# Table powers between projection steps, the convolution in 14 of 16 slots, a wait ahead of the expert splits

## The reference

```
h = rms_norm(x, g_mix);  z = h @ w_in
c_val, c_gate, s_in = z[:, :512], z[:, 512:1024], z[:, 1024:]
y_conv = silu(layer_norm(causal_conv31(c_val * sigmoid(c_gate)) + conv_b))
y_ssm  = s5_ssm(s_in, ...)      # 32 groups of 16 channels, 64 complex states each
x = x + [rms_norm(y_conv), rms_norm(y_ssm)] @ w_out
x = x + hierarchical_moe(rms_norm(x))     # 4 groups x 8 experts, top 2, SwiGLU
return rms_norm(x, g_final)
```

## Time and profile before

| | |
|---|---|
| median of 3 runs | 1887.34 us (1884.49 to 1889.06) |
| profiled execution | 1895.12 us, of it 1893.7 in the span of the trace |
| PE busy | 1640.9 us, 87% of the span |
| DVE, ACT, POOL busy | 1116.7 (59%), 803.3 (42%), 605.9 (32%) |
| mean granted PE clock | 0.924 of full speed |
| stages, from the trace | projection to 360, convolution and state space to 545, mix to 918, experts to 1847, final norm to the end |

### The profile page before, as it was taken

The page is one execution under the profiler, slowest core; times in us unless marked ns, Lnnn a source line. Parts: engine busy times, 40 slices in busy tenths (PEclk is TensorE's granted clock), DMA queues, the critical chain, the costliest instruction groups (busy, mean ns, idle before and its releaser), DMA issues. The chain is left out here.

```text
span 1893.7 us, 33245 instructions
## 1 busy us (share of the span) xinstructions
PE 1640.9 (87%) x11171; PEld 1500.2 (79%) x11172; DVE 1116.7 (59%) x1707; ACT 803.3 (42%) x1022; POOL 605.9 (32%) x882
## 2 busy tenths in 40 slices
PE   7699999688937999999269999999999999999970
PEld 7599999577827888888268999899999888989860
DVE  7845564244547566665617646654666886665546
ACT  3222221012245333342315646644665775665543
POOL 0776774222323336444311212121222121212120
PEclk9899999878968898989579999999999999999995
DMA  8544342498854224312539878885877999887749
GB/s 278 169 146 147 127 161 85 121 223 247 225 200 137 97 89 134 101 67 90 215 119 316 275 240 272 274 285 188 291 273 257 382 366 359 280 275 254 261 137 366
DMA packets 166974, 403.90 MB, mean 213 GB/s; under 512 B 67967, under 2 KB 103169, under 8 KB 140417
## 3 DMA queue, kind: packets, MB, share of 16 engines
q1 hardware_dynamic: 140320, 336.26, 49.7%
q0 software_dynamic: 20080, 58.34, 12.7%
q10 hardware_dynamic: 6512, 8.51, 1.4%
HBM read 313.92 MB, written 89.13 MB: 213 GB/s over the span
## 5 line engine op out<-in xcount | busy, mean ns | idle before, releaser
L1637 DVE TENSOR_TENSOR expert_lo<-expert_raw,expert_hi 128x2048 fp32r<-128x2048 f32 x192 | 430.5, 2284 | 46.4 <-ACT expert_hi L1633 44.6
L1633 ACT CAST expert_hi<-expert_raw 128x2048 fp32r<-128x2048 f32 x192 | 361.6, 1910 | 18.1 <-DMA expert_raw<-in_experts 9.8
L720 PE MATMUL proj_p_z<-proj_x_hi,proj_w_hi 128*128 128x256 f32 x768 | 222.2, 289 | 14.1 <-DVE proj_x_lo L553 14.1
L721 PE MATMUL proj_p_z<-proj_x_lo,proj_w_hi 128*128 128x256 f32 x768 | 218.7, 285 | 0.0
L722 PE MATMUL proj_p_z<-proj_x_hi,proj_w_lo 128*128 128x256 f32 x768 | 218.5, 285 | 0.0
L2037 PE MATMUL moe_p_g0u<-expert_hi,moe_xh 128*128 128x256 f32 x736 | 210.8, 286 | 1.5 <-DVE moe_xl L1950 1.5
L2039 PE MATMUL moe_p_g0u<-expert_lo,moe_xh 128*128 128x256 f32 x736 | 206.6, 281 | 0.0
L2038 PE MATMUL moe_p_g0u<-expert_hi,moe_xl 128*128 128x256 f32 x736 | 206.6, 281 | 0.0
L2052 PE MATMUL moe_p_y<-expert_hi,moe_hh 128*128 128x512 f32 x368 | 153.4, 417 | 13.1 <-DVE moe_hl L1961 13.1
L1879 POOL DMA_INDIRECT residual<-moe_y,moe_ids_s x46 | 78.5, 1708 | 265.6 <-ACT moe_y L1906 258.1
L720 PEld LDWEIGHTS proj_p_z<-proj_x_hi,proj_w_hi 128*128 128x128 f32 x768 | 148.9, 194 | 14.2 <-issue 14.1
(11 more groups left out here) (416 smaller groups left out, 4149.9 us busy)
## 6 DMA issues: line engine op xcount, KB each, us to landing
expert_raw<-in_experts SPq DMA_DIRECT2D x192, 1024.0 KB, 6.2
ffn_input<-mix_h SPq DMA_DIRECT2D x17, 512.0 KB, 3.9
proj_x_sb<-in_x SPq DMA_DIRECT2D x8, 1024.0 KB, 7.3
mix_x_sb<-in_x SPq DMA_DIRECT2D x16, 512.0 KB, 5.0
residual<-mix_x SPq DMA_DIRECT2D x16, 512.0 KB, 2.7
out<-final_x SPq DMA_DIRECT2D x16, 512.0 KB, 6.4
proj_x_raw<-in_x_turned SPq DMA_DIRECT2D x7, 1024.0 KB, 4.8
proj_w_raw<-in_w_in SPq DMA_DIRECT2D x8, 768.0 KB, 7.3
```

The source lines that it names most:

```text
L720: nc.tensor.matmul(o, whi, x_hi[:, half, c], start=start, stop=False)
L721: nc.tensor.matmul(o, whi, x_lo[:, half, c], start=False, stop=False)
L1633: self.nc.scalar.copy(self.hi[:, u], self.raw[:, u]).then_inc(self.hi_done, 1)
L1637: tensor_tensor(self.lo[:, u], self.raw[:, u], self.hi[:, u].bitcast(FP32), ALU.subtract).then_inc(self.lo_done, 1)
```

## The change

It has three parts. No arithmetic changes, and no operation is added or left out, but the eight signed copies of the powers move from DVE to ACT.

**Projection.** `table_factors` is split: `powers` runs after `low(2)` and `factors(2)`, ahead of the scaling of step 1; ACT makes the signed copies (`signed_powers`); `scaled_b` runs after step 1. All loops are written out. The group t of unit j in step n is now `t = (n - 2) * 6 + j - 2`: tables begin at unit 2 of step 2. `expand` follows the scaling of the unit with a pair's second group, and `skip_lag` follows the scaling of the unit after that, which for a pair in units 4 and 5 is unit 0 of the next step.

```diff
+        def group_at(n, j):
+            t = (n - FIRST) * UNITS + j - FIRST_UNIT
+            return t if 0 <= t < GRP else None
...
+            def signed_powers():
+                act.wait_ge(powers_done, 1)
+                ...
+                    last = nc.scalar.activation(to[half].rearrange("p g j -> p j g"), of[half], ACT.Copy, scale=float(sign))
+                last.then_inc(signed, 1)
...
             def factors(n):
                 dve.wait_ge(squared, n * 2 + 2)
+                wait(dve, spread, n)
...
+            def body(n, half):
+                if 1 < n < T8 - 1:
+                    low(n + 1, 1 - half)
+                    factors(n + 1)
+                for j in range(UNITS):
+                    if j >= 4:
+                        glu(n, j - 4)
+                    scaled(n, half, j)
+                    t = group_at(n, j)
+                    if t is not None and t % PAIR == PAIR - 1 and t + 1 < GRP:
+                        expand(t // PAIR + 1)
+                    before = group_at(n, j - 1) if j else group_at(n - 1, UNITS - 1)
+                    if before is not None and before % PAIR == PAIR - 1:
                         for g in range(PAIR):
+                            skip_lag(before // PAIR, g)
                 for j in (2, 3):
                     glu(n, j)
-            body(0, 0, False, 0)
-            table_factors()
-            body(1, 1, True, 0)
-            expand(0, 0)
+            body(0, 0)
+            low(2, 0)
+            factors(2)
+            powers()
+            body(1, 1)
+            scaled_b()
+            dve.wait_ge(signed, 1)
+            expand(0)
+            for n in range(2, T8):
+                body(n, n % 2)
```

```diff
+        TWICE = (5, 9)
+        banks_in = [[0]]
+        for m in range(1, SLOTS):
+            after = banks_in[-1][-1] + 1 if banks_in[-1] else CT * BANKS
+            banks_in.append(list(range(after, min(after + (2 if m in TWICE else 1), CT * BANKS))))
...
+            load_in(0)
             load_u(0)
-            load_column(nc, sp, bias[:, :], conv_b).then_inc(b_in, 16)
-            load_in(0)
             sp.wait_ge(tables_st, 16 * TB)
             load_toep(0)
...
             load_toep(1)
+            sp.dma_start(bias[:, :], conv_b).then_inc(b_in, 16)
             load_u(2)
...
             for m in range(SLOTS):
-                bank(m)
+                for i in banks_in[m]:
+                    bank(i)
...
             act.wait_ge(b_in, 16)
             for m in range(SLOTS):
-                copy_bank(m)
-                if m % BANKS == 2 and m > 2:
-                    finish(m // BANKS - 1)
+                for i in banks_in[m]:
+                    copy_bank(i)
+                if tile_ending(m - 2) is not None:
+                    finish(tile_ending(m - 2))
                 copy_y(m)
-            finish(CT - 1)
```

```diff
-            pool.sem_inc(entries_issued, 1)
             pool.wait_ge(scattered_last, 16 * 2 * LT)
...
-            dve.wait_ge(entries_issued, 1)
+            dve.wait_ge(scattered_last, 16 * 2 * LT)
```

More of the change, by code:

```diff
@@ L368, in _, with body @@
             u_v = scratch["u"].rearrange("(c p) s k -> s p c k", p=P)
-            def body(n, half, more, pairs):
+            def body(n, more):
                 if more:
@@ L375, in body @@
                 sp.dma_start(s_v[n], s_out[:, :, :]).then_inc(s_stored, 16)
-                for k in range(pairs):
-                    store_pair((n - FIRST) * PER_STEP + k, (half + k) % 2)
+                for j in range(UNITS):
+                    t = group_at(n, j)
+                    if t is not None and t % PAIR == PAIR - 1:
+                        store_pair(t // PAIR)
                 sp.wait_ge(u_done, n * CT + CT)
                 sp.dma_start(u_v[n], u_out[:, :, :]).then_inc(u_stored, 16)
[L381 to L388, removed]
+            for n in range(T8):
+                body(n, n < T8 - 2)
+            sp.wait_ge(st_pair, 64 * GRP // PAIR)
             sp.wait_ge(s_stored, 16 * T8)
@@ L456, in body @@
                         gate(n, j - 2)
-                    if j == 3 and more is not None:
+                    if j == 3 and n + 1 < T8:
                         spread_factor(n + 1, 1 - half)
-                    if j < pairs * PAIR:
-                        copy_tables(j % PAIR, (n - FIRST) * PER_STEP + j // PAIR)
-            body(0, 0, False, 0)
-            body(1, 1, True, 0)
[L464 to L468, removed]
+                    t = group_at(n, j)
+                    if t is not None:
+                        copy_tables(t % PAIR, t // PAIR)
+                if n == 0:
+                    high(2, 0)
+                    square(2, 0)
+                    signed_powers()
+            for n in range(T8):
+                body(n, n % 2)
         @block.gpsimd
@@ L576, in glu, with powers @@
                 V.tensor_tensor(u_out[:, j], z[:, j % 2, 0:NK], z[:, j % 2, NK:2 * NK], ALU.mult).then_inc(u_done, 1)
[L578 to L587, removed]
+            factors_step = Chain(dve, factors_own)
+            def powers():
+                step = factors_step
                 step(V.memset(pw_re[:, 0, :], 1.0))
@@ L613, in table_factors, with expand @@
                 complex_mul(V, step, bb[:, 0], bb[:, 1], q_re, q_im, b_raw[:, 0], b_raw[:, 1], tmp[:, 0], tmp[:, 1])
[L616 to L623, removed]
+            def expand(m):
                 def of_pair(ap, pattern):
                     return ap.rearrange(pattern, g=PAIR)[:, bass.ds(m, 1)].squeeze(1)
-                if not isinstance(m, int) or m >= 2:
+                parity = m % 2
+                if m >= 2:
                     dve.wait_ge(products_done, PAIR * m - PAIR)
@@ L753, in table_products, with products @@
                                  start=True, stop=True).then_inc(products_done, 1)
-            def products(n, half, more, pairs):
+            def products(n, half):
                 pe.wait_ge(lo_done, n + 2)
```

100 lines of the change are left out of this document (40 added, 60 removed).

## The result

The changed kernel is slower: median 1893.33 us (1892.3 to 1902.35, 7 runs) against 1885.58 (1882.15 to 1889.06, 7 runs), ratio 1.0055 with a 95% interval of 1.0036 to 1.0075. That is 8 us more, where 15 less was predicted, and the time lies above the range (1857 to 1883). The profiled execution took 1892.47 us, 1891.0 of it in the span: near its own median. The one of before was 9.5 above its own (1895.12), so the two traces differ by -2.7 where the medians differ by +7.8, and a difference between them has to be read stage by stage.

The account below looks back on a forecast made before the run. PE was taken to bound projection and experts, loads in turn with PE the convolution stage. Terms -17 + 10 - 2 - 6 = -15 off the median of 1887.3 gave 1872.3 us, range 1857 to 1883 (8 in 10).

Parts of the forecast that it names:

- The stall of step 1: Projection: PE's 15.1 us wait for step 2's row factors and the slow restart after it go; -17 us.
- The stall at step 2's first table: Projection: PE may wait in unit 2 of step 2 for DVE's first table; up to 2 us.
- The order between steps: Projection: the later skip term makes PE wait for ACT's table copy, mainly in steps 3 and 6; +10 us (3 to 28).
- rival 2: Projection: the skip term makes PE wait at every step, four starts at 7 each, +28 us, time 1890; chance 0.07.
- my case: Whole kernel: the main forecast, 10 to 20 us gained; chance 0.5.
- Convolution stage: Stage between projection and experts: its three edits together give -2 us.
- (a): Convolution stage: block 0's inputs first and bias in 128 pieces start the first state step earlier; -1 us (0 to -1).
- (b): Convolution stage: the bias behind the second Toeplitz load delays ACT's first copy and PE; +3 us (0 to +7).
- Rival 3: Convolution stage: the bias lands after 412 behind full queues, costing +7 or more, time 1879; chance 0.13.
- (c): Convolution stage: banks moved to earlier slots shorten the tail, though bank 12 waits for its matrices; -4 us (-9 to 0).
- Experts: Experts: with DVE waiting for the scatters, these end sooner and PE starts earlier; -6 us (-1 to -7.5).
- Rival 4: Experts: DVE's six subtractions keep POOL from issuing the gather until 957, gaining 0 there, time 1878; chance 0.1.

Follow-up runs that it names:

- e5: Changed kernel with the skip term back ahead of the factors and the bias loaded third in the convolution stage; 0.9928 of the kernel before.
- e7: Changed kernel with the skip term ahead of the factors, bias loaded third, one bank in each of 16 slots; 0.9911 of the kernel before.
- e10: Kernel before with the change's convolution stage, but the bias loaded third; 1.0029 of the kernel before.
- e12: e9_pause with SP's loads of expert 1 also held until the first block's rows have landed; 0.9884 of the kernel before.
- e13: Kernel before with block 0's inputs loaded first, then the first convolution tile, then the bias contiguously, banks as before; 0.9987 of the kernel before.
- e6: Changed kernel with the skip term ahead of the factors, bias still late, one bank in each of 16 slots; 0.9948 of the kernel before.
- e8: Changed kernel with the skip term ahead of the factors, bias third, banks doubled in slots 7 and 11, not 5 and 9; 0.9878 of the kernel before.
- e9_pause: e8 with DVE doing two of expert 0's six subtractions, then splitting the first block's rows, then the other four; 0.9884 of the kernel before.

## Why the prediction was wrong

**The stall of step 1, -17.** Right. PE comes to the factors of step 2 at 79.5 and not at 93.8, without a wait, and the half clock after it is gone: 14.2 and some 1.8, -16. The stall at step 2's first table, which I had allowed up to 2, took 2.9; it is counted in the next term here. With the skip term in its old place, projection ends 11.8 sooner; the rest of the 16 are the new waits of step 2 and small ones after it.

**The order between steps, +10.** The mechanism was right, and this is the first step that failed, by its size: +23, or +20 without the 2.9 of step 2's first table. PE's distance from one spreading of factors to the next is 41.95 in an undisturbed step. In the changed kernel it is 48.0 for step 3 (+6.1), 42.5 for step 4 (+0.6), 43.8 for step 5 (+1.8) and 52.0 for step 6 (+10.0); the wait of 2.9 in step 2 and the last two steps make it 23. The first and last were named, at 4.8 plus a restart and at 2 to 4 plus one. Step 3 came near in the sum, by luck: ACT's copy cost 1.9 and not 4.8, and 1.2 for an expansion, 0.8 for ACT's copy in step 2 and 2.3 of half clock made up for it. But step 6 had 6.9 of waiting and 3 of half clock: POOL's long operations of 128x508 (to 281.8) lay on `glu`, the remainder and the factors together, as at the worst start, where I had taken them to lie on some of these. And I asked about POOL's long operations only at the starts of steps, and only for ACT's copy. `expand`, now a unit later, made PE wait itself where such a stretch lay on it (1.2 each at 142.3, 246.1 and 313.8). I had put steps 4 and 5 at 0 to 0.5 each. The end of rival 2, a late start at every step, was thus nearer than my case: 23 of its 28 us, from two bad starts and several small ones. The run with the skip term moved back wins 18.8 in the stage; some 14 of them are the two waits for ACT's copy and the half clock behind them, so that edit is the main cause. The place of `expand` has no run of its own. Writing out the loops costs nothing, as said: there an undisturbed step takes 41.94.

**Convolution stage, -2.** This is the second step that failed; the part alone costs 9. The bias stayed inside its own bounds, at twice its size, and the banks went the other way.

(a) The inputs first, -1: measured at -2.4, within its uncertainty.

(b) The bias, +3 (0 to +7): measured at some +6. The places came out as I said: ACT's first copy at 412.9, which is 405.9 counted back to the old stage's start (7.0 earlier), PE idle ahead of bank 2, and no wait ahead of block 2. I took off the 4.1 that PE waited for block 2's weights, as if the bias could hide behind that. But this wait was the longest of four traces of the old stage (none, 2.4, 2.5 and 4.1), and with the inputs first and the bias early it is 0 to 1.8 in seven (e5, e7 to e10, e12, e13): there was little to hide behind. Whether edit (a) took this slack is not shown, since block 2's loads are issued 47.9 to 51.6 us into the stage with it and 49.5 to 53.0 without. Rival 3, the bias holding the stage, came nearer here than my case: it had the stage at +5. Its condition, the bias landing after 412, was not met, and it cost some 6 even so.

(c) The banks, -4 (-9 to 0): some +5 by the timed runs, +1 by the traces, and a gain in no pair of runs. The 4 between the two are not explained. The tail was right: from block 7's issue to the mix's first issue 43 to 45 us became 37 to 39. But block 7's loads are issued when slot 11's output products are done, and the two extra banks (3.6 each) and the wait for bank 12's matrices (3.3, in slot 10 as predicted) all stand ahead of these. The distance from block 3 to block 7 grew by 6.7 (85.5 in the mean of five traces with the new places, 78.8 in that of seven with one bank in each slot, e6 with 80.2 among them). I had written that the two banks could leave PE's path, and did not ask which load the slots behind them release. Slots 7 and 11 of e8 show the other case: there PE waited for weights anyway (6.6 and 2.3), the distance is 79.2 in the mean of three traces, as with one bank in each slot, and the tail is 35 to 36.

**Experts, -6.** Right in size: 6.2 in the pair of traces, 8.5 (3.6 to 13.2) by the run alone; from the first of the eight scatters to the first product 34.3 to 35.8 in the six traces without the wait, 26.6 to 28.1 in the eight with it and no loads held. One step was off: the gather did not keep its old pace of 4.4, but DVE's subtractions (to 962.9) covered most of what it lost. Rival 4, the gather locked out by DVE's subtractions, fell: the gather was issued amid them, and in `e9_pause` DVE was idle for most of it, and it took as long. The Trainium skill's rule (SBUF — State Buffer, section "SBUF: two separate sides") is borne out by the issue alone, 2.3 us beside a subtraction against 1.0. Of the 4.4 by which the rows are late, 1.3 are this and some 3 the loads of expert 1.

**The sum.** -16 + 23 + 9 - 8.5 gives +7.5 from the runs by parts; +8 to +10 was measured. I had all four mechanisms, and rival 2's place, but gave rival 2 a chance of 0.07 and bounded it at +3 by keeping the convolution stage at -2. Both failed terms erred in the same direction: both counted on slack, time that could be lost without making anyone wait, which the trace of the old kernel showed and the new one did not have. What stays open is how the 9 us of the convolution part are shared out: its single traces (190.1 to 198.9 from the end of projection to the mix's first issue, old 189.1 to 197.6) show only about half of them. The spread of the stage from run to run hides the rest, or it lies in the stages behind.

## What to carry to other kernels

An edit that puts a short operation behind a long chain on its engine must be followed through all who wait for it, for every start of the loop with what the other engines run at that time, and it should be priced at the worst start seen, not the mean. When work is moved to an earlier slot, look first for the slot whose end releases the next loads: ahead of it the work delays these loads, unless the engine waits there anyway. Here the work cost nothing in the slots with such a wait, and of all versions tried those built on that are the fastest, e8 with 0.9878 (0.9843 to 0.9913) of the kernel before. Slack read from one trace is no reserve: the wait that the bias was to hide behind was 0 to 4.1 us in four traces of the same stage.

## What I had not expected of the hardware

Equal executions of the old kernel spread over 20 us (1874.31 to 1894.86 in the 35 beside the runs by parts), at mean granted clocks from 0.925 to 0.934, the slow ones mostly at the low end. Two traces of it differ by 11.4 us over all stages. So a single trace can't show a change of 8 us in this kernel except in a stage that repeats itself to some 2 or 3 us, as projection does (352.6 to 354.8 for PE's end in six traces of its old form). A gather of 128 rows took 4.3 to 4.5 us with the large loads over, 5.7 with them held but its issue beside a subtraction, and 8.1 to 9.7 with loads of 1 MB issued around it.
